# Head and tail of a one-layer encoder step: norms by a diagonal matmul, the gain on the weights, the last row tile in halves

## What is computed

```python
h  = rms_norm(x, g_mix)                  # x * rsqrt(mean(x*x) + 1e-6) * g_mix
q, k, v, u, g = split(h @ w_in)          # 1024 -> 1792 columns
y  = x + concat([attention(q, k, v), gmlp(u, g)]) @ w_out
y  = y + (silu(rms_norm(y, g_ffn) @ w_gate) * (rms_norm(y, g_ffn) @ w_up)) @ w_down
out = rms_norm(y, g_final)
```

## Time and profile before

| | |
|---|---|
| median of three runs | 1033.73 us |
| profiled execution, time | 1034.63 us |
| profiled execution, span | 1032.9 us |
| TensorE busy | 1004.6 us, 97% |
| VectorE, GpSimd, ScalarE busy | 626.1, 409.4, 387.8 us |
| HBM traffic over the span | 150 GB/s |

### The profile page before, as it was taken

How to read it: one execution, slowest core, us unless ns; L and a number is a source line. 1 busy time by engine, 2 the same in 40 slices (tenths; PEclk the granted TensorE clock), 3 DMA queues, 4 the chain that set the end, 5 groups by cost and what they waited for, 6 DMA issues and landing times.

```text
span 1032.9 us, 16272 instructions
## 1 busy us (share of the span) xinstructions
PE 1004.6 (97%) x5754; PEld 835.9 (81%) x5754; DVE 626.1 (61%) x874; ACT 387.8 (38%) x698; POOL 409.4 (40%) x445
## 2 busy tenths in 40 slices
PE   5999999999999899999999999999999999999996
PEld 4999998888887787787787787887877777777885
DVE  5475637766255696676766567667764647535725
ACT  5411144445223443333333333333333446234431
POOL 2011100000000367696696777877973400202055
PEclk9999999999999999999999999999999999999999
DMA  8311331100321434553643643644637999388814
GB/s 277 102 45 43 84 85 43 43 2 8 133 86 67 148 112 131 158 173 105 187 149 112 193 146 110 208 138 123 184 114 233 325 347 381 138 301 303 292 41 168
DMA packets 166130, 155.84 MB, mean 151 GB/s; under 512 B 16224, under 2 KB 129280, under 8 KB 166080
## 3 DMA queue, kind: packets, MB, share of 16 engines
q1 hardware_dynamic: 166080, 155.16, 46.8%
HBM read 114.17 MB, written 41.06 MB: 150 GB/s over the span
## 4 chain that ended last, share of the span: by engine, by line
PE 84%; DMA 6%; DVE 5%; POOL 2%; ACT 1%; issue 1%; SPq 1%; POOLq 0%; ACTq 0%; DVEq 0%
PE ps L1095 26%; PE ps L1096 25%; PE ps L1097 25%; DMA xd_in<-act_scratch 3%; PE ps L1381 2%; PE ps L1132 2%; DMA act_scratch<-act_sums 1%; PE ps L1267 1%; PE ps L1245 1%; DMA out_state_gmlp_v_sample<-work 1%; PE ps L1229 1%; DMA act_scratch<-ffn_blocks_even 1%; DVE work L1959 1%; PE ps L1469 1%; DVE ln_st L1953 1%
## 5 line engine op out<-in xcount | busy, mean ns | idle before, releaser
L1095 PE MATMUL ps<-x_forms,w_forms 128*128 128x512 f32 (+1 forms) x644 | 246.4, 383 | 4.5 <-DVE w_forms L1874 3.0
L1096 PE MATMUL ps<-x_forms,w_forms 128*128 128x512 f32 (+1 forms) x644 | 244.7, 380 | 0.0
L1097 PE MATMUL ps<-x_forms,w_forms 128*128 128x512 f32 (+1 forms) x644 | 244.6, 380 | 0.0
L1095 PEld LDWEIGHTS ps<-x_forms,w_forms 128*128 128x128 f32 x644 | 121.1, 188 | 32.8 <-issue 6.8
L1097 PEld LDWEIGHTS ps<-x_forms,w_forms 128*128 128x128 f32 x644 | 121.1, 188 | 23.0
L1096 PEld LDWEIGHTS ps<-x_forms,w_forms 128*128 128x128 f32 x644 | 121.1, 188 | 22.4
L1095 PE MATMUL ps<-w_dn,x_dn 128*128 128x512 f32 x308 | 121.6, 395 | 0.8 <-DVE y_acc_sample L2338 0.8
L1097 PE MATMUL ps<-w_dn,x_dn 128*128 128x512 f32 x308 | 120.0, 389 | 0.0
L1096 PE MATMUL ps<-w_dn,x_dn 128*128 128x512 f32 x308 | 119.9, 389 | 0.0
L947 POOL TENSOR_SCALAR meansq<-sumsq 128x1 f32<-128x1 f32 (+1 forms) x27 | 10.8, 400 | 257.1 <-ACT xn_ffn L1517 227.0
L1874 DVE TENSOR_TENSOR w_dn<-wd_in,w_dn 128x1024 fp32r<-128x1024 f32 (+1 forms) x42 | 49.3, 1175 | 80.1 <-ACT w_dn L1805 79.0
(11 more groups left out here) (246 smaller groups left out, 2089.7 us busy)
## 6 DMA issues: line engine op xcount, KB each, us to landing
xd_in<-act_scratch SPq DMA_DIRECT2D x35, 512.0 KB, 7.9
t_raw<-in_w_down SPq DMA_DIRECT2D x88, 128.0 KB, 2.6
act_scratch<-act_sums SPq DMA_DIRECT2D x22, 512.0 KB, 4.4
y_acc_odd<-in_w_down SPq DMA_DIRECT2D x22, 512.0 KB, 6.4
wd_in<-t_scratch SPq DMA_DIRECT2D x20, 512.0 KB, 7.7
wd_in<-in_w_down SPq DMA_DIRECT2D x15, 512.0 KB, 6.5
stage<-in_w_in SPq DMA_DIRECT2D x28, 256.0 KB, 3.6
w_stage_even<-in_w_gate SPq DMA_DIRECT2D x22, 256.0 KB, 3.3
```

The lines of the kernel that those rows point to most:

```text
L1095: mm(out, wh, xh, start=first, stop=False, skip_group_check=onto)
L1096: mm(out, wh, xl, start=False, stop=False, skip_group_check=onto)
L1097: return mm(out, wl, xh, start=False, stop=last, skip_group_check=onto)
```

## The change

The norm of the head is split. The gain g_mix is no longer multiplied onto the rows but onto the rows of w_in: it is loaded as 8 rows of 128 numbers, turned by one transpose, and kept as one column per 128 input rows; each unit is multiplied with it in its stage buffer, unit 0 by VectorE, units 1 to 13 by GpSimd, and the split of a unit waits for that. The first three tiles are not normalised by VectorE at all: it multiplies the identity by the column of norms, and TensorE multiplies the loaded rows with that diagonal, which turns and scales them at once. For the other tiles VectorE multiplies by the norm alone. The squares of tiles 0 to 5 write their unused product to PSUM and so wait for no turn. The list is reordered. TensorE makes 26 transposes of the identity ahead of the first tile and 8 behind the third. The load and the mask of the spatial weights move behind tile 8. In the tail, tiles 3 and 5 (the norms of `i` = 6 and 7 in the order above) are normalised before the last `add_tile`; the last tile is squared in halves, its upper half takes the gain ahead of the last sum, ScalarE multiplies that half by the norm while VectorE does the lower one, and each half is stored by itself.

```diff
+DIAGONAL = 3
+EARLY_SQUARES = 6
...
+LAST_TILE = LAST_ORDER[-1]
...
-    s = [("front", 0), ("front", 1), ("back", 0), ("front", 2), ("split", 0), ("back", 1),
-         ("front", 3), ("back", 2), ("split", 1), ("front", 4), ("back", 3), ("front", 5),
-         ("block", 0, 0), ("back", 4), ("front", 6), ("block", 0, 1), ("back", 5), ("front", 7),
-         ("evac", 0), ("block", 1, 0), ("back", 6), ("front", 8), ("block", 1, 1), ("back", 7),
-         ("evac", 1), ("block", 2, 0), ("back", 8), ("block", 2, 1), ("evac", 2),
-         ("block", 3, None), ("evac", 3), ("block", 4, None), ("evac", 4), ("split", 2),
-         ("block", 5, None), ("evac", 5), ("split", 3)]
+    s = [("front", 0), ("front", 1), ("front", 2), ("gain",), ("scale", 0), ("back", 0), ("back", 1),
+         ("split", 0), ("back", 2), ("scale", 1), ("front", 3), ("front", 4), ("split", 1),
+         ("block", 0, 0), ("front", 5), ("back", 3), ("block", 0, 1), ("front", 6), ("back", 4),
+         ("evac", 0), ("block", 1, 0), ("front", 7), ("back", 5), ("block", 1, 1), ("scale", 2), ("back", 6),
+         ("evac", 1), ("block", 2, 0), ("front", 8), ("back", 7), ("block", 2, 1), ("back", 8), ("evac", 2),
+         ("block", 3, None), ("evac", 3), ("block", 4, None), ("evac", 4), ("split", 2), ("scale", 3),
+         ("block", 5, None), ("evac", 5), ("split", 3), ("scale", 4)]
...
+            if t + 3 < N_PROJ:
+                s.append(("scale", t + 3))
...
+        last_sq = sb("last_sq", [P, 2])
+        last_mean = sb("last_mean", [P, 1])
+        g_mix_rows = sb("g_mix_rows", [KT, P])
+        g_mix = sb("g_mix", [P, KT])
...
+        def scale_unit(eng, n):
+            w = unit_stage(n).rearrange("p (k c) -> p k c", k=KT)
+            return eng.tensor_tensor(w, w, g_mix[:, :].unsqueeze(2).to_broadcast([P, KT, P]), ALU.mult)
...
             def load_rows(i):
-                if i >= 4:
+                if 4 <= i < 4 + DIAGONAL:
+                    sp.wait_ge(turned, i - 3)
+                elif i >= 4:
                     sp.wait_ge(xn_ready, i - 3)
...
             load_rows(0)
-            sp.dma_start(gain[:, :], a["g_mix"][0].partition_broadcast(P)).then_inc(gain_landed, 16)
             load_rows(1)
+            sp.dma_start(g_mix_rows[:, :], a["g_mix"][0].rearrange("(k p) -> k p", p=P)).then_inc(g_mix_landed, 16)
             load_rows(2)
...
             load_unit(1)
-            sp.dma_start(wsp, a["gmlp_w_spatial"][0].rearrange("g t s -> t g s")).then_inc(wsp_landed, 16)
             load_rows(4)
...
             load_rows(8)
+            sp.dma_start(wsp, a["gmlp_w_spatial"][0].rearrange("g t s -> t g s")).then_inc(wsp_landed, 16)
             sp.dma_start(ln_g, a["gmlp_ln_g"][0].partition_broadcast(P)).then_inc(small_landed, 16)
...
-            for r in range(2 * ROWS, 3 * ROWS):
+            for r in range(2 * ROWS, 3 * ROWS - 1):
...
+            sp.wait_ge(last_scaled, 1)
+            sp.dma_start(y_rows[LAST_TILE][:, 512:D], y_acc_row(LAST_TILE)[:, 512:D]).then_inc(y_out, 16)
+            sp.wait_ge(xn_ready, 3 * ROWS)
+            sp.dma_start(y_rows[LAST_TILE][:, 0:512], y_acc_row(LAST_TILE)[:, 0:512]).then_inc(y_out, 16)
...
-            sp.wait_ge(y_out, 16 * ROWS)
+            sp.wait_ge(y_out, 16 * (ROWS + 1))
...
-                    if item == ("front", 4):
-                        pool.wait_ge(tril_ready, 1)
...
-                if item == ("back", 2):
+                if item[0] == "scale" and item[1] >= 1:
+                    unit_landed(pool, item[1])
+                    pool.wait_ge(g_mix_ready, 1)
+                    pool.wait_ge(unit_scaled, item[1])
+                    scale_unit(nc.gpsimd, item[1]).then_inc(unit_scaled, 1)
+                if item == ("back", 8):
...
-                    pool.wait_ge(rstd_ready, 4)
+                    pool.wait_ge(rstd_ready, ROWS)
...
-                        pool.wait_ge(rstd_ready, ROWS)
+                        pool.wait_ge(tril_ready, 1)
...
-            for i in range(ROWS):
+            for i in range(ROWS - 1):
...
+            last = 3 * ROWS - 1
+            pool.wait_ge(rstd_ready, last)
+            pool.wait_ge(meansq_ready, last + 1)
+            nc.gpsimd.tensor_tensor(rstd[:, last:last + 1], meansq[:, last:last + 1], neg_half[:, 0:1],
+                                    ALU.pow).then_inc(rstd_ready, 1)
...
-                if r == 0:
-                    pe.wait_ge(pool_consts, 6)
...
                 for k in range(KT):
-                    t = turn(out[:, k, 0:n], src[:, P * k:P * k + P], ident[rows, rows])
+                    if r < DIAGONAL:
+                        t = mm(out[:, k, :], xin[:, i % 4, P * k:P * k + P], xn[:, i % 2, 0:P], start=True, stop=True)
+                    else:
+                        t = turn(out[:, k, 0:n], src[:, P * k:P * k + P], ident[rows, rows])
                 t.then_inc(turned, 1)
+            def idle_turns(n):
+                for _ in range(n):
+                    turn(ps[:, 1, 0:P], ident[:, :], ident[:, :])
+            def turn_gain():
+                pe.wait_ge(g_mix_landed, 16)
+                turn(ps[:, 0, 0:KT], g_mix_rows[:, :], ident[0:KT, 0:KT]).then_inc(g_mix_turned, 1)
...
+            pe.wait_ge(pool_consts, 6)
+            idle_turns(26)
             for item in SCHEDULE:
...
                     norm_back(item[1])
+                    if item[1] == 0:
+                        turn_gain()
+                    if item[1] == 2:
+                        idle_turns(8)
                 elif kind == "block":
...
-                if 2 <= r < ROWS:
+                if 1 <= r < EARLY_SQUARES:
+                    act.wait_ge(sumsq_ready, r)
+                elif EARLY_SQUARES <= r < ROWS:
...
-                dst = xn[rows, i % 2, :] if r < ROWS else xn_ffn[rows, :] if r < 2 * ROWS else squares(r)
+                if r < EARLY_SQUARES:
+                    dst = ps[:, 2:4, :].rearrange("p b c -> p (b c)")
+                else:
+                    dst = xn[rows, i % 2, :] if r < ROWS else xn_ffn[rows, :] if r < 2 * ROWS else squares(r)
...
+            def keep_gain():
+                act.wait_ge(g_mix_turned, 1)
+                nc.scalar.copy(g_mix[:, :], ps[:, 0, 0:KT]).then_inc(g_mix_ready, 1)
...
-                unit_landed(act, n)
+                if n < N_PROJ:
+                    act.wait_ge(unit_scaled, n + 1)
+                else:
+                    unit_landed(act, n)
...
                     norm_front(item[1])
+                elif kind == "gain":
+                    keep_gain()
                 elif kind == "back":
...
-            for i in range(ROWS):
+            for i in range(ROWS - 1):
...
+            def last_squares(h):
+                act.wait_ge(sumsq_ready, 3 * ROWS - 2)
+                if h == 1:
+                    act.wait_ge(resid_used, 2 * TILES)
+                else:
+                    act.wait_ge(c21_added, TILES)
+                nc.scalar.activation(ps[:, 2 + h, :], y_acc_row(LAST_TILE)[:, 512 * h:512 * h + 512], ACT.Square,
+                                     accum_out=last_sq[:, h:h + 1]).then_inc(last_squared, 1)
+            last_squares(1)
+            last_squares(0)
+            act.wait_ge(last_begun, 2)
+            act.wait_ge(rstd_ready, 3 * ROWS)
+            y = y_acc_row(LAST_TILE)[:, 512:D]
+            nc.scalar.activation(y, y, ACT.Copy, scale=rstd[:, 3 * ROWS - 1:3 * ROWS]).then_inc(last_scaled, 1)
...
-                src = xin[rows, i % 4, :] if r < ROWS else y_row(r - ROWS) if r < 2 * ROWS else y_acc_row(i)
+                if r < ROWS:
+                    if r == 0:
+                        dve.wait_ge(pool_consts, 6)
+                    if r >= 2:
+                        dve.wait_ge(turned, r - 1)
+                    dve.wait_ge(rstd_ready, r + 1)
+                    src, dst = xin[rows, i % 4, :], xn[rows, i % 2, :]
+                    if r < DIAGONAL:
+                        src, dst = ident[:, :], xn[:, i % 2, 0:P]
+                    nc.vector.tensor_scalar(dst, src, rstd[rows, r:r + 1], None, ALU.mult).then_inc(xn_ready, 1)
+                    return
+                src = y_row(r - ROWS) if r < 2 * ROWS else y_acc_row(i)
...
-                    dve.wait_ge(gain_landed, 16 * (r // ROWS + 1))
+                    dve.wait_ge(gain_landed, 16 * (r // ROWS))
...
-                dst = xn[rows, i % 2, :] if r < ROWS else xn_ffn[rows, :] if r < 2 * ROWS else src
+                dst = xn_ffn[rows, :] if r < 2 * ROWS else src
...
                     norm_front(item[1])
+                elif item == ("scale", 0):
+                    unit_landed(dve, 0)
+                    dve.wait_ge(g_mix_ready, 1)
+                    scale_unit(nc.vector, 0).then_inc(unit_scaled, 1)
                 elif kind == "back":
...
-            for t in range(TILES):
-                add_tile(STAGES - 1, t)
-                norm_front(2 * ROWS + 2 * t)
-                norm_front(2 * ROWS + 2 * t + 1)
-            norm_front(3 * ROWS - 1)
```

(32 more changed lines are left out.)

## The result

| | before | after |
|---|---|---|
| median | 1033.80 us (6 runs) | 1038.41 us (6 runs, 1037.32 to 1040.72) |
| ratio | | 1.0043, 95% interval 1.003 to 1.0056 |
| profiled execution: time, span | 1034.63, 1032.9 | 1038.33, 1036.6 |
| TensorE, VectorE, GpSimd busy | | 1013.3, 632.0, 434.6 |

The account below looks back on a forecast made before the run. TensorE was taken as the bound, busy 1004.6 of 1032.9 us, leaving gains at the two ends. Head 1.8 plus tail 1.6 gave 3.4 us off the 1033.73 median: 1030.3 us, range 1028.4 to 1032.7.

Parts of the forecast that it names:

- Head up to the first block: Kernel start: first projection block starts at 16.8 us against 19.81 before, bounds 15.6 to 17.5.
- The matmul with a diagonal counts as a turn: Head, first three tiles: a diagonal matmul costs 1.97 us on the slow clock, some 0.86 on the fast.
- The stall: Before block (2,0), row tiles 3 to 5: TensorE waits 1.8 us for tile 5's low part, starting at 30.5.
- I take 1.28: Head, tile 7's norm without gain on VectorE: 1.28 us, with ends 0.69 and 2.3.
- 2.3 as an end: Rival, longer stall: tile 7's norm takes 2.3 us, block (2,0) one us later, time 1031.3; 8%.
- The aside on the one-input op: Tile 7's norm, by the skill: about 0.65 us alone, 1.2 when colliding with GpSimd, sum unchanged.
- Gaps of 2.5 us in the new head should not bring it down: Head: TensorE gaps of 2.5 us leave the clock up, judging by the earlier tail.
- up for the first block: Head sum assumes full clock at the first block; rival that it stays down: head gives 0.6, time 1031.5, 18%.
- I take nothing: Between head and tail: GpSimd's 12 later scalings cost 0 us, bounds 0 and 1.1 each.
- The rival of held-back scalings: Between 40 and 200 us: scalings delay VectorE and TensorE waits, up to 13 us, 1043 in all; 12%.
- Tail: After the last matmul: last store issue ends at 1028.5 instead of 1030.13, 1.6 us less, bounds 1.0 and 2.0.
- Sum: Whole kernel: head 1.8 plus tail 1.6 gives 3.4 us less; profiled execution to come to 1031.2.

Follow-up runs that it names:

- e5: Changed kernel, with GpSimd's scaling of unit 2 waiting until VectorE has made tile 5's low part; median 1035.13 us, ratio to before 1.0013.
- e11: Kernel before with the tail's part, plus idle transposes in its old head (26 ahead of the first tile; 12, 12, 20 behind tiles 0 to 2); median 1030.89 us.
- e9: The changed kernel run once more, unaltered; median 1038.04 us, ratio to before 1.0038.
- e4: Changed kernel, with the store of the first normalised rows moved ahead of the stage load in SyncE's queue; median 1036.55 us, ratio to before 1.002.
- e1: Kernel before with only the change's parts for the last tile; median 1032.44 us, ratio to before 0.9984.
- e8: Changed kernel, tile 5's low part before tile 7's norm, unit 2's scaling after it, units 5 to 7 scaled earlier, store before load; median 1031.86 us.
- e12: e8 with diagonal matmuls for tiles 0 and 1 only, and unit 1's scaling behind unit 0's low part; median 1031.16 us, ratio to before 0.9981.
- e2: Changed kernel, with GpSimd's scaling of unit 2 moved behind tile 8's norm statistics in the list; median 1040.79 us, ratio to before 1.007.

## Why the prediction was wrong

- **Head up to the first block.** 16.8 foretold, 17.48 came, inside the bounds. Tile 2 landed later, its square starting at 8.06 instead of 7.5, and the third diagonal was ready at 10.6 instead of 9.9. Unit 0's low part took 1.93 instead of 2.3, GpSimd's scaling 1.90 instead of 2.6. "The matmul with a diagonal counts as a turn" failed: it is recorded as 16 for 8 and takes 2.05 us warm, so tile 2's high part came at 16.1, and VectorE, free at 15.8, waited 0.28 for it.
- **The stall, the step that failed first.** The profiled execution came out 7.1 us above the 1031.2 foretold for it, and here the larger part begins. I put 1.8 us and block (2,0) at 30.5; it was 2.9 and 32.47. About 1.0 of the 2.0 late is the head's lateness carried along, 1.0 the norm: "I take 1.28". The norm is 0.75 alone and 2.31 held (e5, after). The text saw that GpSimd starts on unit 2 "at that very moment" and named 2.3 as an end, and gave it 8%. With the collision certain by its own times, that end was the forecast. The aside on the one-input op, 0.65 alone and 1.2 when it collides, was near for the first and far off for the second, and that the sum would not change was wrong.
- **The clock.** "Gaps of 2.5 us in the new head should not bring it down" rested on the earlier trace rows, a gap with nothing behind it. After the 2.9 us stall it fell in three of four profiles, for a loss of 1.6 us in the first. That it is up for the first block was right. The Trainium skill's rule on transposes ("TensorE: Matmul & The Clock Gate", Part 4: PE-mode transpose), which would have kept it down, does not hold here: in e11 the 26 transposes themselves go from 0.21 to 0.11 us apart, by 6.9 us, with no real matmul before them. The measurement decides.
- **Between the ends: "I take nothing".** It cost 1.3 us (e9) to 3.2 (the first profile, with its fall). The bound of 1.1 for each scaling was too low, 1.63 for the one that mattered; but what I missed is the chain of queue and store that carries VectorE's lateness to TensorE, shown by e4. The rival of held-back scalings, at 12%, named "the mixing of positions" as the place, and was right.
- **Tail.** 1.6 foretold, 1.7 in the profile, 1.9 in the median of e1: right by its steps, with the half norm 0.75 for 0.69.
- **Sum.** -1.8 became +1.95, 0 became +3.2, +0.3 came later, -1.6 became -1.7: the profiled execution moved by 3.7 us.

## What to carry to other kernels

Work given to GpSimd is not free because it has time: its ops on SBUF held those VectorE ops with all operands in SBUF that came behind them until they had ended (2.31 us for 0.75, 4.76 through three of them), so put them beside VectorE ops that read PSUM (1.22 with and without), and look which VectorE op starts next in the trace. Before a change with four parts is judged, try its cheapest part alone: 70 idle transposes in the old head (e11) gave at least as much as the diagonals, the scalings and their idle transposes together, placed as well as I could (e8, e12). And where an engine has slack, follow its lateness through the queues as well; a store behind a load turned 1.6 us of VectorE into 1.2 to 1.6 of TensorE.

## What the runs showed that was not expected

- A 32x1024 VectorE op, the sample's norm, stood for 4.76 us in e2, through two GpSimd scalings and a mask between them. The 1.21 that it takes in e8 is a wait too: it ends 0.54 after the mask. Timeline of e8:

```profile
34.23 1.21 DVE L1984 TENSOR_SCALAR work<-work,rstd 32x1024 f32<-32x1024 f32 x1 [2.65 <-POOL rstd L979]
34.26 0.64 POOL L996 TENSOR_SCALAR_AFFINE_SELECT work<-work 128x512 f32<-128x512 f32 x1
34.86 2.34 POOL L578 TENSOR_TENSOR stage<-stage,g_mix 128x1024 f32<-128x1024 f32 x1
```

- Here VectorE's op came ahead of the next scaling, and that took 2.34 us instead of 1.90: GpSimd is held as well.
- Of the nine affine ops in the chain above, one was held, the first: it begins 0.08 us behind the scaling and ends at 98.76, when that has ended (98.61); the others take their 0.34. VectorE's timeline after, the first op of that row:

```profile
96.79 1.97 DVE L2063 SCALAR_TENSOR_TENSOR work<-work,ln_rstd 128x128 f32<-128x128 f32 x1 [0.54 <-POOL ln_rstd L1006]
```

- The granted clock reads 1.00 in the cold start, though 384 columns take 0.32 us (1.2 GHz), and 0.50 in a later fall with the same pace.
- VectorE's one-input product of 128x1024 takes 0.75 us, against 1.28 with the gain.
